# An inference step of a pooling and sparse-attention decoder: VectorE's steps reordered in the chosen-key loop, and block loads asked for one tile later

## The chip, the cores and the metric

The kernel is one program on 1 core of one Trainium2 chip. A core has TensorE (PE in the profile; its weight loads are PEld), VectorE (DVE), ScalarE (ACT), GpSimd (POOL) and SyncE (SP). Each takes its own instructions in the order written and they meet only at semaphores. SP, ScalarE and GpSimd also issue DMAs. The metric is the device time of one execution in microseconds, lower is better: 1763.3 us, the median of 3 runs (1761.06 to 1765.92).

## What is computed

One decoder layer works on 512 prompt rows and 8 sample rows (520 columns once transposed). The input is projected, pooled, attended in three branches, gated, merged, projected out and normalised. Cut to what matters here:

```python
h = x @ w_in + b_in              # u | z_pool | q | kv (6 parts) | gates | z_nsa | merge gates
# pooling: trailing means over 2, 4, 8, 16 positions, minus the token
c = cumsum(u);  m = (c[i] - c[i - w]) / min(pos + 1, w) - u
y_pool = (m per group @ pool_w) * pool_scale
# sparse attention of the 8 sample rows
p_cmp = masked_softmax(q . compressed_keys)           # 64 compressed blocks
score = p_cmp summed over the 4 heads of a group, and over 2 blocks; first and current block forced
idx   = top_k(score, 16)                              # 16 blocks of 64 keys
o_sel = softmax(q . k[idx]) @ v[idx]
o_win = softmax(q . window_keys) @ window_values      # 512 keys
o = g0 * o_cmp + g1 * o_sel + g2 * o_win
a = (y_pool * silu(z_pool)) @ w_up_pool;  b = (o * silu(z_nsa)) @ w_up_nsa
y = layer_norm(ALPHA * x + (sigmoid(gA) * a + sigmoid(gB) * b) @ w_out)
```

## The kernel before

**Units.** Every large projection is cut into units of 128 output columns. A weight tile (128x2048 f32, 1 MB) is loaded by SP into `wst`, ScalarE rounds it to `wh` (`split_hi`, L654), VectorE forms the remainder `wl` (`split_lo`, L659), and TensorE does three passes for each of 16 slices and two halves of the rows: 96 matmuls (L671 to L673). Two buffers alternate. A unit may be done in 8 parts of 12 matmuls, and `fill(count)` puts so many parts wherever TensorE would otherwise wait.

**The chosen-key loop.** The sample rows' attention runs in 48 steps t, between the parts of filler units. Steps 0 to 23 (`K_END`) are keys: 0 to 7 (`W_END` is 8) are window keys, 8 to 23 chosen keys, two steps to a sample row. Steps 24 to 47 are values. One key step is, on TensorE, `turn_keys(t)` (8 transposes, L938), `fill(FILL[t])` (2 or 3 parts) and `score_keys(t)` (4 matmuls, L955). After the transposes ScalarE rounds the turned keys (`out_keys`, L1343), VectorE subtracts (`out_keys`, L1678), and only then may `score_keys(t)` go. `ended(t)` names the filler unit that TensorE finishes in step t: this is one in the steps 0, 2, 5, 9, 12, 14, 17, 20 and 23, and none in the others. There `end_unit` does ScalarE's `split_hi` of the unit after next and the output of the ended one, and VectorE's `split_lo`; `split_hi` waits until TensorE has used the old weights.

**Other work in these steps.** VectorE ranks the blocks (`rank_blocks` at t = 1, `choose_blocks` at t = 3). At t = 5 it waits for TensorE's row of block offsets, copies it (L1818) and signals `gather_ready`, for which SP, GpSimd and ScalarE wait before they load the first chosen tile. From t = 8 it does the pooling of one u tile in two steps (`pool_tile`: even t the first half, odd t the second), and at t = 9 a chain of small operations, `row_gain` (L1734 to L1743).

**Chosen tiles.** Tile f is used by `turn_keys(f)` and lies in buffer f % 4. It consists of blocks of 64 rows, 32 KB each and two heads: SP and GpSimd issue six each, ScalarE the rest (`load_rest`: four for even f, two for odd f). ScalarE's issues stand between its `out_keys(t)` and its `end_unit`. The order of everything is written out by hand.

**The start.** After x has been turned and split, TensorE turns the first cache pages (L734, `turn_pages`), for which it waits for the semaphores `t_evac`, then begins unit 0.

Of the kernel before, what the change touches and what calls it, by code (L numbers as in the profile page):

```python
# [64 lines left out]
def build(nc, x_prompt, x_sample, cache_cmp_k, cache_cmp_v, cache_slc_k, cache_slc_v, cache_win_k,  # L65
# [5 lines left out]
    with ExitStack() as ctx:  # L71
        def sem(name):
            return ctx.enter_context(nc.semaphore(name))
# [114 lines left out]
        t_evac = [sem("t_evac0"), sem("t_evac1")]  # L188
# [59 lines left out]
        W_END, K_END, VW_END, V_END = 8, 24, 32, 48  # L248

        def parts_before(t):  # L250

            return 8 + sum(FILL[:t]) + (SEAM if t >= K_END else 0)

        def unit_fill(k):

            return k % 2, k // 2 + 27 - k % 2

        def ended(t):

            after = parts_before(t) + FILL[t] + (SEAM if t == K_END - 1 else 0)  # L260
            return range(parts_before(t) // 8 if t else 0, after // 8)
# [15 lines left out]
        def load_chosen(eng, regs, cache, n, h, first, last, signal):  # L277

            slot, base = n % 4, n // 2 * 32 + h * 16 + n % 2 * 8
            eng.load(regs[0:last - first], row_offs.bitcast(I32)[:, base + first:base + last])  # L280
            for r in range(first, last):
                at = eng.snap(regs[r - first], min_val=0, max_val=2 * NPHYS - 1)
                eng.dma_start(stage8[r % 2 * 64:r % 2 * 64 + 64, slot, r // 2, h * HD:(h + 1) * HD],
                              blocks_of(cache)[bass.ds(at, 1), :, h, :].rearrange("o p d -> p (o d)")
                              ).then_inc(signal[slot], 16)
# [363 lines left out]
        def split_hi(act, b, n, first=False, k=KD):  # L649

            act.wait_ge(w_in_s[b], n * 16 + 16)
            if not first:
                act.wait_ge(w_used[b], n)
            act.activation(wh[:, b, 0:k], wst[:, b, 0:k], ACT.Copy).then_inc(w_hi[b], 1)  # L654

        def split_lo(dve, b, n, k=KD):

            dve.wait_ge(w_hi[b], n + 1)
            dve.tensor_tensor(wl[:, b, 0:k], wst[:, b, 0:k], wh[:, b, 0:k].bitcast(F32), ALU.subtract).then_inc(w_lo[b], 1)  # L659
# [457 lines left out]
        def _(act):  # L1117
# [8 lines left out]
            for k in range(KD):  # L1126
# [2 lines left out]
            act.wait_ge(x_tr, KD + 2)  # L1129
            act.activation(xh[:, :, SEQ:ROWS], pb[5][:, 0:KD * NB].rearrange("p (k b) -> p k b", b=NB), copy  # L1130
                           ).then_inc(x_hi, 1)
            split_hi(act, 0, 0, first=True)
            act.sem_inc(phase, 1)

# [10 lines left out]

            for b in range(2):
                act.sem_inc(evac[b], 1)
            act.sem_inc(t_evac[1], 1)
            act.sem_inc(c2_evac, 1)
            for b in range(2):  # L1150
                act.sem_inc(spilled[b], 1)
# [173 lines left out]
            def load_rest(cache, n, last=8):  # L1325

                for h in range(NKV):
                    load_chosen(act, block_regs, cache, n, h, 6, last, k_in)
# [9 lines left out]
            def out_keys(t):  # L1338
                if t > 0:
                    act.wait_ge(sk_done, t)  # L1340
                for h in range(NKV):
                    act.wait_ge(kt_ready[h], t + 1)
                    act.activation(khl[:, 0, h, :], pb[4 + h][:, :], copy).then_inc(kh_ready, 1)  # L1343

            def move_low(bank, cols, scored):

                act.wait_ge(sk_done, scored)
                act.activation(S[:, cols], pb[bank][64:P, 0:cols.stop - cols.start], copy).then_inc(lo_moved, 1)
# [22 lines left out]
            for t in range(K_END):  # L1371
                if t == W_END:
                    move_low(6, slice(1024, 1536), W_END)
                out_keys(t)
                if t == 6:
                    act.wait_ge(gather_ready, 1)
                    load_rest(cache_slc_k, 0)
                if 6 <= t < K_END - 3:
                    load_rest(cache_slc_k, t + 3 - W_END, 8 - (t + 3) % 2)
                if t == K_END - 1:  # L1380
                    move_low(6, slice(0, 512), K_END - 1)
                    turned_hi(pTw, 5, WPG, 1)
                    values_hi(K_END)
                    move_low(7, slice(512, 960), K_END)
                for k in ended(t):
                    end_unit(k)
                if t == W_END:
                    exps(1, slice(1024, 1536), 1)
# [73 lines left out]
        def _(dve):  # L1462

            for k in range(KD):
# [3 lines left out]
            dve.wait_ge(x_hi, KD + 1)  # L1468
            dve.tensor_tensor(xl[:, :, SEQ:ROWS], pb[5][:, 0:KD * NB].rearrange("p (k b) -> p k b", b=NB),
                              xh[:, :, SEQ:ROWS].bitcast(F32), ALU.subtract).then_inc(x_lo, 1)  # L1470
            split_lo(dve, 0, 0)
            dve.sem_inc(phase, 1)

# [9 lines left out]
                last.then_inc(evac[b], 1)  # L1483


            dve.sem_inc(t_evac[0], 1)
            def compress_sequence(kv, r, par, first=False):
                n = r * 2 + (kv * NB + par)

# [179 lines left out]
            def end_unit(k):  # L1669
                b, n = unit_fill(k)  # L1670
                split_lo(dve, b, n + 1)
                if k >= 8:
                    silu_tile(u[:, k, :], b, k, k - 7)
# [125 lines left out]
            for t in range(K_END):  # L1799
                if t == W_END:  # L1800
                    add_high(6, slice(1024, 1536), 1)
                out_keys(t)
                if t == K_END - 1:
                    add_high(6, slice(0, 512), 2)
                    turned_lo(pTw, 5, WPG, 1)
                    dve.tensor_copy(wm[:, 8:16], pb[5][:, 256:264])
                    dve.drain().then_inc(pl_ready, 1)
                    values_lo(K_END)
                    add_high(7, slice(512, 960), 3)
                for k in ended(t):  # L1810
                    end_unit(k)
                if t == 1:
                    rank_blocks()
                if t == 3:
                    choose_blocks()
                if t == 5:
                    dve.wait_ge(step, C + 12)
                    dve.tensor_copy(row_offs.bitcast(I32), pb[7][0:1, 0:256])  # L1818
                    dve.drain().then_inc(gather_ready, 1)
                    dve.tensor_copy(osum, pb[7][:, 320:384])  # L1820
                    dve.drain().then_inc(step, 1)
                if t == W_END:
                    row_max(1, slice(1024, 1536))
                if t == W_END + 1:
                    row_gain(1, 1)
                if t >= W_END:
                    pool_tile((t - W_END) // 2, (t - W_END) % 2 == 1)
            for t in range(K_END, V_END):
                if t + 1 < V_END:
                    values_lo(t + 1)  # L1830
                if t - 1 >= K_END and (t <= VW_END or t % 2 == 0):
                    add_values(t - 1)
                if t == K_END:
                    row_max(0, slice(0, 960))
                if t == K_END + 4:
                    row_gain(0, 2)
                if t == K_END + 6:
                    turned_lo(pTs, 6, 8, 2)
                    dve.tensor_copy(wm[:, 0:8], pb[7][:, 128:136])
                    dve.drain().then_inc(pl_ready, 1)  # L1840
                if t == K_END + 7:
                    for kind in range(2):
                        dve.tensor_tensor(newv[:, kind * 64:kind * 64 + 64].rearrange("p (x g) -> p x g", g=G),
                                          pb[7][:, kind * 64:kind * 64 + 64].rearrange("p (x g) -> p x g", g=G),
                                          by_head(vnew, kind), ALU.mult)
                    dve.drain().then_inc(new_evac, 1)
                    for kind in range(2):
                        dve.tensor_tensor(osum, osum, newv[:, kind * 64:kind * 64 + 64], ALU.add)
                        dve.drain()
                for k in ended(t):  # L1850
                    end_unit(k)
                if t == VW_END + 7:
                    dve.wait_ge(sums_ready, 1)
                    dve.tensor_tensor(ssum, pb[6][:, 0:64].rearrange("p (c b) -> p c b", b=NB), u[:, 0:8, SEQ:ROWS], ALU.add)
                    dve.drain()
                    for g, w in enumerate(POOL_W):
                        new = u[:, 2 * g:2 * g + 2, SEQ:ROWS]
                        last = dve.scalar_tensor_tensor(new, ssum[:, 2 * g:2 * g + 2, :], 1.0 / w, new, ALU.mult, ALU.subtract)
                    last.then_inc(diff_ready, 1)
# [180 lines left out]
```

## Time and profile before

| What | Value |
|---|---|
| Median of 3 runs | 1763.3 us (1761.06 to 1765.92) |
| The profiled execution | 1766.08 us, of which the span is 1764.6 |
| Mean granted TensorE clock | 0.983 |
| PE busy | 1710.6 us (97% of the span) |
| DVE busy | 738.0 us (42%) |
| ACT busy | 582.7 us (33%) |
| POOL busy | 165.7 us (9%) |

Busy time is the time in which at least one instruction of the engine was running. The rows shown further down are from the same execution; all starts are microseconds from the start of its span. A row of the timeline gives the start, the duration in us, engine, line, operation, output and inputs, the count, and in brackets how long the engine had been idle before and whose end released it. ACTq, DVEq and the like are an engine's sequencer, which issues DMAs. The key steps 5 to 23 lie between 1026 and 1150 us.

### The profile page before, as it was taken

The numbers are of one execution on the slowest core, as the hardware profiler recorded it, in microseconds if no ns is written. First come the engines' busy times: TensorE is split into PE (matmuls) and PEld (weight loads), VectorE is DVE, ScalarE is ACT, GpSimd is POOL, SyncE is SP. The second block draws the span as 40 slices with busy tenths as digits, with TensorE's granted clock in tenths as the row PEclk, the third lists the DMA queues.
The fourth block names the chain that finished last, engine by engine and source line by source line (L and its number), as shares of the span: only waits on it lengthen the run. The fifth ranks groups of instructions, "written<-read, shape, count | busy, mean of one in ns | idle before, by whom it ended". The sixth has DMA issues, their size and how long they took to land.

```text
span 1764.6 us, 35960 instructions
## 1 busy us (share of the span) xinstructions
PE 1710.6 (97%) x13797; PEld 1662.1 (94%) x13797; DVE 738.0 (42%) x1169; ACT 582.7 (33%) x830; POOL 165.7 (9%) x320
## 2 busy tenths in 40 slices
PE   7999999999999998999999999989999999999996
PEld 6999999999999998998989988889999999999996
DVE  4333323222222113444544446564353444455685
ACT  4433333331222213333333332354232333343331
POOL 0000000000000010000000135236200000000000
PEclk9999999999999987999999999999999999999998
DMA  9555655544444254222322646456633444577783
GB/s 280 156 156 148 191 160 146 151 142 148 140 128 123 71 147 124 72 75 63 85 66 60 209 122 160 127 156 153 173 82 91 144 138 137 140 210 217 203 243 103
DMA packets 354262, 248.87 MB, mean 141 GB/s; under 512 B 16893, under 2 KB 336835, under 8 KB 353378
## 3 DMA queue, kind: packets, MB, share of 16 engines
q1 hardware_dynamic: 330114, 205.28, 41.6%
q0 software_dynamic: 15104, 38.81, 7.0%
q10 hardware_dynamic: 8960, 3.68, 0.8%
q8 instruction: 50, 0.82, 0.2%
q14 instruction: 34, 0.28, 0.1%
HBM read 229.50 MB, written 27.03 MB: 145 GB/s over the span
## 4 chain that ended last, share of the span: by engine, by line
PE 55%; DVE 3%; ACT 1%; DVEq 1%; issue 1%; ACTq 1%; PEldq 0%; PEld 0%
PE bank L671 8%; PE bank L672 8%; PE bank L673 8%; PE bank L1079 3%; PE bank L1080 3%; PE bank L1081 3%; PE bank L687 3%; PE bank L688 3%; PE bank L689 3%; PE bank L867 2%; PE bank L955 1%; PE bank L938 1%; DVE wl L659 1%; PE bank L851 1%; PE bank L837 1%; PE bank L839 1%
## 5 line engine op out<-in xcount | busy, mean ns | idle before, releaser
L671 PE MATMUL bank<-xh,wh 128*128 128x260 f32 x1952 | 563.2, 289 | 1.3 <-DVE wl L659 1.0
L672 PE MATMUL bank<-xl,wh 128*128 128x260 f32 x1952 | 553.2, 283 | 0.0
L673 PE MATMUL bank<-xh,wl 128*128 128x260 f32 x1952 | 552.9, 283 | 0.0
L659 DVE TENSOR_TENSOR wl<-wst,wh 128x2048 fp32r<-128x2048 f32 (+1 forms) x141 | 289.0, 2049 | 353.9 <-ACT wh L654 353.7
L671 PEld LDWEIGHTS bank<-xh,wh 128*128 128x128 f32 x1952 | 369.7, 189 | 2.7 <-DVE wl L659 1.2
L672 PEld LDWEIGHTS bank<-xl,wh 128*128 128x128 f32 x1952 | 369.7, 189 | 0.0
L673 PEld LDWEIGHTS bank<-xh,wl 128*128 128x128 f32 x1952 | 369.5, 189 | 0.0
L654 ACT ACTIVATE wh<-wst 128x2048 fp32r<-128x2048 f32 (+1 forms) x141 | 243.2, 1725 | 129.2 <-PE bank L673 101.8
L687 PE MATMUL bank<-xh,wh 128*128 128x260 f32 x512 | 155.3, 303 | 0.0
L1079 PE MATMUL bank<-xh,wh 128*128 128x264 f32 (+1 forms) x512 | 147.3, 288 | 0.0
L688 PE MATMUL bank<-xl,wh 128*128 128x260 f32 x512 | 145.2, 284 | 0.0
L689 PE MATMUL bank<-xh,wl 128*128 128x260 f32 x512 | 145.2, 284 | 0.0
L1081 PE MATMUL bank<-xh,wl 128*128 128x264 f32 (+1 forms) x512 | 144.4, 282 | 0.0
L672 PE MATMUL bank<-yl,wh 128*128 128x260 f32 x512 | 144.4, 282 | 0.0
L673 PE MATMUL bank<-yh,wl 128*128 128x260 f32 x512 | 144.3, 282 | 0.0
L671 PE MATMUL bank<-yh,wh 128*128 128x260 f32 x512 | 144.3, 282 | 0.0
L1080 PE MATMUL bank<-xl,wh 128*128 128x264 f32 (+1 forms) x512 | 144.3, 282 | 0.0
L754 PE MATMUL bank<-xt,w 128*128 128x128 f32 (+1 forms) x1024 | 118.2, 276 | 0.0
L754 PEld LDWEIGHTS bank<-xt,w 128*128 128x128 f32 x1024 | 115.6, 192 | 1.6
L644 ACT ACTIVATE xt<-bank 128x512 f32<-128x512 f32 x64 | 75.7, 1183 | 105.9 <-PE bank L734 105.7
L643 DVE COPY xt<-bank 128x512 f32<-128x512 f32 x64 | 73.7, 1152 | 82.7 <-PE bank L734 82.7
L687 PEld LDWEIGHTS bank<-xh,wh 128*128 128x128 f32 x512 | 97.4, 190 | 3.1 <-issue 1.9
(320 smaller groups left out, 2350.2 us busy)
## 6 DMA issues: line engine op xcount, KB each, us to landing
wst<-in_w_in SPq DMA_DIRECT2D x77, 1024.0 KB, 5.7
wst<-in_w_out SPq DMA_DIRECT2D x32, 1024.0 KB, 6.0
stage<-in_cache_cmp_k SPq DMA_DIRECT2D x128, 128.0 KB, 2.2
stage<-in_cache_cmp_v SPq DMA_DIRECT2D x128, 128.0 KB, 2.1
merge_gates<-sig POOLq DMA_DIRECT2D x32, 260.0 KB, 2.3
sig<-merge_gates POOLq DMA_DIRECT2D x32, 260.0 KB, 2.9
wst<-in_w_up_pool SPq DMA_DIRECT2D x16, 512.0 KB, 4.3
wst<-in_w_up_nsa SPq DMA_DIRECT2D x16, 512.0 KB, 4.2
```

What stands on the lines that cost most here:

```text
L654: act.activation(wh[:, b, 0:k], wst[:, b, 0:k], ACT.Copy).then_inc(w_hi[b], 1)
L659: dve.tensor_tensor(wl[:, b, 0:k], wst[:, b, 0:k], wh[:, b, 0:k].bitcast(F32), ALU.subtract).then_inc(w_lo[b], 1)
L671: pe.matmul(bank[:, 0:HALF], wh[:, b, k, :], hi[:, rows], start=(at == 0), stop=False)
L672: pe.matmul(bank[:, 0:HALF], wh[:, b, k, :], lo[:, rows], start=False, stop=False)
L673: last = pe.matmul(bank[:, 0:HALF], wl[:, b, k, :], hi[:, rows], start=False, stop=end)
L687: pe.matmul(bank, wh[:, b, k, :], xh[:, k, rows], start=(k == 0), stop=False)
L688: pe.matmul(bank, wh[:, b, k, :], xl[:, k, rows], start=False, stop=False)
L689: last = pe.matmul(bank, wl[:, b, k, :], xh[:, k, rows], start=False, stop=(k == KD - 1))
L754: last = pe.matmul(pb[6][:, 0:width], w1[:, j, :], xt[:, par, j, 0:width], start=(j == 0), stop=(j == CB - 1))
L1079: pe.matmul(bank[:, 0:width], wh[:, b, k, :], xh[:, k, rows], start=(k == 0), stop=False)
L1080: pe.matmul(bank[:, 0:width], wh[:, b, k, :], xl[:, k, rows], start=False, stop=False)
L1081: last = pe.matmul(bank[:, 0:width], wl[:, b, k, :], xh[:, k, rows], start=False, stop=(k == KD - 1))
```

## The change

Three edits. In VectorE's key loop, `end_unit` is moved from before the ranking, copying, `row_gain` and pooling work of the step to after it. In ScalarE's key loop, the rest of tile f is asked for in step f - 2 and no longer in step f - 3; tile 8's rest stays in step 6. At the start, the first increments of `t_evac` stand ahead of the first weight split on both engines and no longer behind it.

```diff
@@ scalar
             act.activation(xh[:, :, SEQ:ROWS], ...).then_inc(x_hi, 1)
+            act.sem_inc(t_evac[1], 1)
             split_hi(act, 0, 0, first=True)
...
-            act.sem_inc(t_evac[1], 1)
             act.sem_inc(c2_evac, 1)
@@ scalar, key loop
                 if t == 6:
                     act.wait_ge(gather_ready, 1)
-                    load_rest(cache_slc_k, 0)
-                if 6 <= t < K_END - 3:
-                    load_rest(cache_slc_k, t + 3 - W_END, 8 - (t + 3) % 2)
+                if 6 <= t < K_END - 2:
+                    load_rest(cache_slc_k, t + 2 - W_END, 8 - t % 2)
@@ vector
+            dve.sem_inc(t_evac[0], 1)
             split_lo(dve, 0, 0)
...
-            dve.sem_inc(t_evac[0], 1)
@@ vector, key loop
                     values_lo(K_END)
                     add_high(7, slice(512, 960), 3)
-                for k in ended(t):
-                    end_unit(k)
                 if t == 1:
                     rank_blocks()
...
                 if t >= W_END:
                     pool_tile((t - W_END) // 2, (t - W_END) % 2 == 1)
+                for k in ended(t):
+                    end_unit(k)
```

In the changed file the lines of VectorE's helpers are one lower (L1677 for L1678, L1783 to L1788 for L1784 to L1789, the first half of `pool_tile`). On VectorE at t = 14 and 15, before: keys of 14, weight split, first half of pooling, keys of 15.

```order
L1678 TENSOR_TENSOR khl<-bank,khl 128x512 x2
L659 TENSOR_TENSOR wl<-wst,wh 128x2048
L1784 COPY ukeep<-u 128x23
L1785 COPY u<-u 128x512
L1789 TENSOR_TENSOR u<-u 128x512 x2
L1678 TENSOR_TENSOR khl<-bank,khl 128x512 x2
```

And after, at the same place:

```order
L1677 TENSOR_TENSOR khl<-bank,khl 128x512 x2
L1783 COPY ukeep<-u 128x23
L1784 COPY u<-u 128x512
L1788 TENSOR_TENSOR u<-u 128x512 x2
L659 TENSOR_TENSOR wl<-wst,wh 128x2048
L1677 TENSOR_TENSOR khl<-bank,khl 128x512 x2
```

The split has gone from the front of the pooling to just ahead of the next step's keys. On ScalarE from its `out_keys(9)` to the split of weights in step 9, before:

```order
L1343 ACTIVATE khl<-bank 128x512 [waits kt_ready1]
L280 TENSOR_LOAD kc
L282 ISA
L283 DMA stage<-in_cache_slc_k 64x128
L282 ISA
L283 DMA stage<-in_cache_slc_k 64x128
L280 TENSOR_LOAD kc
L282 ISA
L283 DMA stage<-in_cache_slc_k 64x128
L282 ISA
L283 DMA stage<-in_cache_slc_k 64x128
L654 ACTIVATE wh<-wst 128x2048 [waits w_used1,w_in1]
```

And after:

```order
L1343 ACTIVATE khl<-bank 128x512 [waits kt_ready1]
L280 TENSOR_LOAD kc
L282 ISA
L283 DMA stage<-in_cache_slc_k 64x128
L280 TENSOR_LOAD kc
L282 ISA
L283 DMA stage<-in_cache_slc_k 64x128
L654 ACTIVATE wh<-wst 128x2048 [waits w_used1,w_in1]
```

The odd step now holds two DMAs ahead of the split where it held four; an even step holds four where it held two. TensorE's, GpSimd's and SP's own order is the same in both.

## Rows read from the trace of the kernel before

**Rows 1.** Waits, TensorE's own, 984 to 1165: waiter, releaser, total, times, longest.
```profile
PE bank L955 <- DVE khl L1678: 7.0, 5, 2.2
...
PE bank L1008 <- DVE stage8r L1754: 2.3, 1, 2.3
```

**Rows 2.** Timeline of TensorE: scores of steps 7, 10, 15 and 18.
```profile
1042.48 1.33 PE L955 MATMUL bank<-khl,qm 128*128 128x512 f32 x4 [1.29 <-DVE khl L1678]
...
1063.97 1.33 PE L955 MATMUL bank<-khl,qm 128*128 128x512 f32 x4 [2.24 <-DVE khl L1678]
...
1095.61 1.33 PE L955 MATMUL bank<-khl,qm 128*128 128x512 f32 x4 [1.91 <-DVE khl L1678]
...
1117.16 1.33 PE L955 MATMUL bank<-khl,qm 128*128 128x512 f32 x4 [0.73 <-DVE khl L1678]
```

**Rows 3.** Chain of waits, 1030 to 1046: start, us, what.
```profile
1034.57 0.36 DVEq L1819
...
1038.44 0.64 ACTq L283
...
1041.11 0.60 ACT khl L1343
```

**Rows 4.** Timeline of TensorE, step 5's last matmuls ahead of the offsets.
```profile
1030.17 1.05 PE L962 MATMUL bank<-kc,vc 64*128 64x4 f32 x8
```

**Rows 5.** Timeline of ScalarE, steps 9, 13 and 14.
```profile
1051.83 4.20 ACTq L283 DMA_DIRECT2D stage<-in_cache_slc_k  x4
1056.14 1.92 ACT L654 ACTIVATE wh<-wst 128x2048 fp32r<-128x2048 f32 x1 [4.37 <-issue]
...
1078.56 3.23 ACTq L283 DMA_DIRECT2D stage<-in_cache_slc_k  x4
...
1084.66 1.46 ACTq L283 DMA_DIRECT2D stage<-in_cache_slc_k  x2
1088.60 1.91 ACT L654 ACTIVATE wh<-wst 128x2048 fp32r<-128x2048 f32 x1 [3.69 <-PE bank L673]
```

**Rows 6.** Timeline of VectorE, steps 9 and 10, 14 and 15, 17, 23.
```profile
1058.09 2.29 DVE L659 TENSOR_TENSOR wl<-wst,wh 128x2048 fp32r<-128x2048 f32 x1 [5.60 <-ACT wh L654]
...
1063.22 1.29 DVE L1678 TENSOR_TENSOR khl<-bank,khl 128x512 fp32r<-128x512 f32 x2
...
1090.55 2.29 DVE L659 TENSOR_TENSOR wl<-wst,wh 128x2048 fp32r<-128x2048 f32 x1 [4.81 <-ACT wh L654]
...
1094.86 1.29 DVE L1678 TENSOR_TENSOR khl<-bank,khl 128x512 fp32r<-128x512 f32 x2
...
1112.36 2.29 DVE L659 TENSOR_TENSOR wl<-wst,wh 128x2048 fp32r<-128x2048 f32 x1 [5.16 <-ACT wh L654]
...
1153.31 2.29 DVE L659 TENSOR_TENSOR wl<-wst,wh 128x2048 fp32r<-128x2048 f32 x1 [0.62 <-ACT wh L654]
```

**Rows 7.** Stretches: length, busy of PE, PEld, DVE, ACT, POOL, granted clock, DMA.
```profile
26.00:32.00 6.00, 6.00 (x27) 6.00 (x28) 0.98 (x1) 0.20 (x1) 0.00 (x0) 0.50 0.86 246
1060.00:1070.00 10.00, 7.76 (x54) 6.56 (x53) 6.83 (x20) 1.20 (x2) 7.27 (x15) 1.00 0.49 137
...
1097.00:1101.00 4.00, 4.00 (x23) 4.00 (x22) 2.47 (x8) 1.20 (x2) 1.05 (x2) 0.57 0.78 175
```

**Rows 8.** Line L283, the issues of chosen keys, 984 to 1165.
```profile
DMA to landing us min/median/max: 1.9/2.6/6.4
```

**Rows 9.** Timeline of ScalarE, keys of step 18.
```profile
1112.95 1.08 ACT L1343 ACTIVATE khl<-bank 128x512 fp32r<-128x512 f32 x2
```

**Rows 10.** Timeline of TensorE, transposes of tile 20.
```profile
1123.53 1.04 PE L938 MATMUL bank<-ident,stage 128*128 128x128 f32 x8
```

**Rows 11.** Waits of all engines, 1160 to 1290.
```profile
ACT khl L1368 <- DMA stage<-in_cache_slc_v: 31.2, 10, 5.4
```

**Rows 12.** Timeline of TensorE, the start.
```profile
23.93 1.07 PE L734 MATMUL bank<-ident,stage 128*128 128x128 f32 x8 [2.42 <-DVEq L1486]
26.00 0.58 PE L671 MATMUL bank<-xh,wh 128*128 128x260 f32 x1 [1.00 <-DVE wl L659]
```

## The prediction

> **What bounds the kernel now.** The table of engines comes first: TensorE is busy for 97% of the span and the next engine for 42%, so only what makes TensorE wait, or runs it at a lower clock, moves the end. I then read the waits of TensorE alone over the stretch of the key steps [rows 1]. One line stands out: the score matmuls L955 waited five times for VectorE's `khl`, 7.0 us in all. Just behind the stretch, L1008, the first value products, waited once for 2.3. No wait of TensorE on a tile's DMA is in this answer, so the chosen tiles come in time.
>
> Next, TensorE's timeline around each of the five [rows 2]: 1.29 us at step 7, 2.24 at step 10, 1.91 at step 15, 0.73 at step 18, and by difference from the 7.0 some 0.8 for the fifth, at step 21, which follows the same pattern as step 18. All but step 7 come right after a step in which a filler unit ends (9, 14, 17, 20). That points to `end_unit`.
>
> **Part 1: VectorE's order in the key steps.** Nothing is added or removed; seven splits (steps 5, 9, 12, 14, 17, 20, 23) go behind the other work of their steps. Take step 14 [rows 6]: the split `wl` starts at 1090.55 after 4.81 us of idle time, in which VectorE waited for ScalarE's `wh`. It takes 2.29 us, to 1092.84. Then comes the pooling, to 1094.86, where the keys of step 15 begin. Pooling depends on neither `wh` nor the keys, so it fits into the 4.81 us. With it there, keys 15 start at about 1092.85, 2.0 us sooner, and the score can start at 1093.6. TensorE was ready at 1095.61 - 1.91 = 1093.70 [rows 2]. The stall goes, by a margin of only 0.1.
>
> Steps 17 and 20 have the same shape: idle of 5.16 us ahead of the split at 17 [rows 6], whose end is 1114.65. Keys 18 could then start at once, and the score 0.75 us later (in rows 2 and 6 the score of step 10 starts 1063.97 - 1063.22 = 0.75 after its keys), at 1115.4, against a TensorE ready at 1117.16 - 0.73 = 1116.43. Stall gone, margin 1.0. I take step 20 to be the same, 0.8.
>
> Step 9: the split ends at 1060.38 and `row_gain` with the second half of pooling fill the time to keys 10 at 1063.22 [rows 6]: 2.8 us, which fit into the 5.60 idle ahead. TensorE was ready at 63.97 - 2.24 = 1061.73; keys at 1060.4 mean a score at 1061.15. Gone, margin 0.6 even before part 2.
>
> Step 5: the copy behind `gather_ready` waits for TensorE's offsets, whose matmuls end at 1031.2 [rows 4]. Before, it stood behind the split and its signal came at 1034.57 + 0.36 = 1034.93 [rows 3]. Now it comes at about 1031.2 + 0.4, the same 0.36 with a hand-over, 1031.6: 3.3 us sooner, for ScalarE, SP and GpSimd alike. The first chosen blocks are thus asked for earlier, with the queues of these three empty.
>
> At step 23 the split waited 0.62 for `wh` [rows 6]; 2.5 us of pooling can start in that time, so what follows, up to the values that L1008 awaits, is 0.5 earlier of its 2.3 [rows 1]. Its stall stays at 1.8.
>
> What is late now: `wl` itself, by up to the part of the pooling that doesn't fit. The next use of that buffer lies one whole unit, 8 parts of 12 matmuls, further on, so TensorE doesn't notice; nor does SP, which reloads the buffer after it.
>
> Sum of part 1, with step 7 left to part 2: 2.24 + 1.91 + 0.73 + 0.8 + 0.5 = 6.2 us.
>
> **Part 2: ScalarE's requests.** The count stays 48; each batch of two or four moves one step back. At step 6 ScalarE issued six behind `gather_ready`, and its `khl` began at 1041.11, VectorE's behind it, and the score at 1042.48 [rows 2, 3]. Now it issues four. The first four ended at 1038.44 + 0.64 = 1039.08 [rows 3], and with the signal sooner they can only end sooner. Then the first head's keys 7 on ScalarE, 0.55 (half of 1.08, rows 9), and on VectorE, 0.7 (half of 1.29 and the hand-over, rows 6), and the score may go at 1040.4, against a TensorE ready at 1042.48 - 1.29 = 1041.19. The 1.29 go.
>
> From step 9 on, odd steps issue two and even steps four; before it was the reverse. Step 9 gains: four took 4.20 us and held `wh` until 1056.14 ("issue" is the releaser) [rows 5]. Two save about 2, more margin at step 10. Steps 12, 14 and 20 lose: four take 3.23 in the row of step 13, two take 1.46 at step 14, so 1.8 more in front of `wh`. At 14 the issues would end at 1084.66 + 3.23 = 1087.9, and `wh` waits for TensorE to finish the unit until 1088.60 anyway [rows 5]: hidden, by 0.7. With a batch as slow as that of step 9 (4.20) it would be 0.3 late. So these steps cost from 0 to 0.3 each; I take 0 and keep up to 1 us for the three together.
>
> The price of asking late is the landing. The tightest tile is 20: ScalarE ends keys 18 at 1114.03 [rows 9], four issues bring 1117.4, and the median landing of 2.6 us [rows 8] brings 1120.0. TensorE turns tile 20 at 1123.53 [rows 10]. That leaves 3.5 us, or 2.8 when the 0.73 of step 18 is gone. The longest landing, 6.4, would be late by 1.0. I take 0, bound 1.
>
> Here the Trainium skill speaks against the change: DMA: Bandwidth & Descriptors, Rules for kernel authors, says in effect that a DMA should be issued early and its semaphore waited for late, so that its fixed cost overlaps. By it the later request is at best neutral. The trace has slack of more than a median landing, which is why I give the rule only a small chance; its result is the slower rival below.
>
> Part 2: 1.3 us.
>
> **Part 3: the start.** TensorE's page transposes ran at 23.93, released by VectorE's semaphore increment behind its split, and unit 0 began at 26.00 when `wl` was there [rows 12]. The transposes were already beside the split. They can go sooner, by at most the 2.42 us of idle ahead of them, but the first matmul waits for the same `wl`: 0. What can move is the clock. After the idle stretches of 2.42 and 1.00 it stood at 0.50, the 1.2 GHz level, from 26 to 32 [rows 7]. At half rate 6 us do 3 us of work. Had it stayed at full, 3 us would be won; if it lasted half as long again, 1.5 lost. The idle time is nearly the same, merely more of it in one piece before unit 0; I take 0.
>
> The skill's rule (TensorE: Matmul & The Clock Gate, Part 1) is that a busy engine is given the full clock and an idle one the half, and that the place of the change differs between runs. It gives no sign for this part, and a rival below.
>
> **The clock in the loop.** From 1097 to 1101 the granted clock was 0.57 [rows 7], that is 2 x 0.43 x 4 = 3.4 us at the half level, right behind the 1.91 us stall of step 15. That cost 1.7 us. But the longer stall of step 10 was followed by nothing, 1.00 [rows 7]. So a stall leads to the lower clock sometimes. Without stalls the 1.7 should return, though shifting everything may put another stall, such as the one of 1.8 left at L1008, in its place. Between 0 and 1.7 I take 1.0.
>
> **Sum.** 6.2 + 1.3 + 0 + 1.0 = 8.5 us. The profiled execution took 1766.08, its span 1764.6, and is 2.8 above the median 1763.3, at the upper end of the runs. It would become 1757.6; against the median, 1763.3 - 8.5 = 1754.8 us.
>
> **Rivals.**
> 1. ScalarE's even steps become the bound. Margins of 0.1 and 0.7 at steps 14 and 15 are thin. If four issues there take as long as the slow batch of step 9 and more, `wh`, `wl` and keys 15 are late and part of the 1.91 comes back, with the clock's 1.0: 8.5 - 1.9 - 1.0 - 0.8 (the same at step 21) = 4.8, giving 1758.5. For: rows 5 show a spread of 3.23 to 4.20. Against: only step 9's was so slow, with SP and GpSimd at work in a crowd that now comes earlier.
> 2. The value steps take it back. ScalarE waited ten times, 31.2 us, for chosen values [rows 11]. If those were bound by the rate of DMA, a TensorE that comes 8 us earlier would wait there. Against: TensorE itself shows no such wait, and these loads start by TensorE's own progress. It would leave 1 or 2 us: 1762.
> 3. Slower: rests land late. One tile later, with four issues in the even steps, leaves 2.8 us over the median landing at tile 20. If landings there pass 2.6 + 2.8 = 5.4 us, TensorE waits at its transposes. If seven even tiles waited 2 us each, 14 us against the 8.5: 1763.3 + 5.5 = 1768.8. For: a longest landing of 6.4. Against: a median of 2.6. This is the skill's early-issue rule.
> 4. The clock at the start. With all else as forecast, 3 us either way: 1751.8 at full clock throughout, 1756.3 if the low level lasts longer.
>
> **Chances.** Forecast 0.64, rival 1 0.16, rival 2 0.11, rival 3 0.05, rival 4 0.04. The forecast's own bounds: 6.2 + 1.3 with 1 lost to ScalarE and no clock is 6.5, with the 1.7 of the clock and a little more elsewhere 10.5, and the median itself moves by 1: 1752 to 1758. The range takes in rivals 1 and 4 and runs towards 2: 1750.5 to 1761.5. A change is told from none here from about 0.3%, 5.3 us, so below 1758.0. Faster: nearly all of the forecast and rival 4, and a third of rival 1, 0.72. Slower, above 1768.6: 0.04. The same: 0.24.
>
> **What would show it.** Right: among TensorE's waits, L955 on `khl` falls from 7.0 to under 1; pooling stands before the split, in the idle time; the first chosen DMA is issued at about 1032; the clock is 1.00 from 1060 to 1150. L1008's wait is about 1.8. Part 2 is wrong if TensorE's transposes wait for a DMA, or if ScalarE's `wh` in steps 12, 14 or 20 has "issue" as its releaser with a stall of L955 behind it. The forecast is wrong if the stalls vanish and the time doesn't, for then they were not on the path; or if another stall of like size stands in the value steps.

## The result, and the profile after

| | Before | Changed |
|---|---|---|
| Median | 1763.91 us (5 runs, 1761.06 to 1765.92) | 1753.89 us (5 runs, 1753.21 to 1756.05) |
| Ratio | | 0.9945, 95% interval 0.9934 to 0.9957 |
| Span profiled | 1764.6 us | 1752.0 us |

The change makes the kernel 10.0 us faster by the medians and 0.55% (9.7 us) by the ratio; the forecast was 1754.8. A second set of five runs beside other kernels gave 1755.67 with a ratio of 0.9946 (0.9932 to 0.9959). One execution of the kernel before, beside the second group of experiments below, took 5133 us and is left out of its ratios.

TensorE's waits over the key steps and just behind them in the changed kernel, 984 to 1155, in the columns of [rows 1]:

```profile
PE bank L1008 <- DVE stage8r L1753: 1.6, 1, 1.6
PE bank L1008 <- DVE osacc L1761: 0.6, 1, 0.6
```

The line of L955 with its 7.0 us isn't there any more; L1008 stands at 1.6 where it had 2.3. VectorE's timeline at steps 14 and 15, to be laid beside [rows 6]:

```profile
1078.00 1.29 DVE L1677 TENSOR_TENSOR khl<-bank,khl 128x512 fp32r<-128x512 f32 x2 [2.80 <-ACT khl L1343]
1079.21 0.17 DVE L1783 COPY ukeep<-u 128x23 f32<-128x23 f32 x1
1079.28 0.42 DVE L1784 COPY u<-u 128x512 f32<-128x512 f32 x1
1079.78 1.46 DVE L1788 TENSOR_TENSOR u<-u 128x512 f32<-128x512 f32 x2
1084.06 2.29 DVE L659 TENSOR_TENSOR wl<-wst,wh 128x2048 fp32r<-128x2048 f32 x1 [2.82 <-ACT wh L654]
1086.27 1.28 DVE L1677 TENSOR_TENSOR khl<-bank,khl 128x512 fp32r<-128x512 f32 x2
```

The pooling lies in the idle time ahead of the split, which falls from 4.81 to 2.82 us, and the keys of step 15 follow the split at once. TensorE's score of that step has no bracket, that is, its first matmul did not wait:

```profile
1087.07 1.27 PE L955 MATMUL bank<-khl,qm 128*128 128x512 f32 x4
```

But it took 1.27 us where most take 1.07 to 1.09. A score is two pairs of matmuls, one for each head, and the second pair needs the second half of VectorE's keys. TensorE's weight loads (PEld) show that wait, which the matmul row doesn't:

```profile
1087.60 0.30 PEld L955 LDWEIGHTS bank<-khl,qm 128*128 128x128 f32 x2 [0.30 <-DVE khl L1677]
```

The waits of the weight loads on `khl` from 1026 to 1150, before and changed:

```profile
PEld bank L955 <- DVE khl L1678: 10.0, 12, 2.4
...
PEld bank L955 <- DVE khl L1677: 0.3, 1, 0.3
```

Before, both pairs waited in six steps: the five of [rows 1] and step 6, whose matmul row took 1.33 us without a bracket. In the changed kernel one pair is left, that of step 15.

VectorE in step 5, the copy behind `gather_ready` ahead of the split:

```profile
1029.64 0.41 DVE L1815 CAST kc<-bank 1x256 int32<-1x256 f32 x1 [2.31 <-PE bank L962]
```

ScalarE in steps 6, 9, 12 and 14, to be laid beside [rows 5]:

```profile
1032.53 3.16 ACTq L283 DMA_DIRECT2D stage<-in_cache_slc_k  x4
...
1047.88 1.77 ACTq L283 DMA_DIRECT2D stage<-in_cache_slc_k  x2
1049.75 1.92 ACT L654 ACTIVATE wh<-wst 128x2048 fp32r<-128x2048 f32 x1 [1.73 <-PE bank L673]
...
1065.64 3.11 ACTq L283 DMA_DIRECT2D stage<-in_cache_slc_k  x4
1068.85 1.92 ACT L654 ACTIVATE wh<-wst 128x2048 fp32r<-128x2048 f32 x1 [3.16 <-issue]
...
1078.41 3.10 ACTq L283 DMA_DIRECT2D stage<-in_cache_slc_k  x4
1082.11 1.91 ACT L654 ACTIVATE wh<-wst 128x2048 fp32r<-128x2048 f32 x1 [3.66 <-PE bank L673]
```

Step 9's `wh` is released by TensorE and no longer by the issues. In step 12 it is now the issues that hold it ("issue"), as the price of four in an even step, but no score waits behind. In step 14 the four end at 1081.51, 0.6 ahead of TensorE's release.

The start of each score, read from TensorE's timelines, shows where the time went. A line holds a step, its start in both kernels and by how much the changed kernel is ahead:

| Step | Before | Changed | Ahead | Wait of the step before the change |
|---|---|---|---|---|
| 5 | 1031.15 | 1029.53 | 1.6 | |
| 7 | 1042.48 | 1039.00 | 3.5 | 1.29 |
| 9 | 1055.46 | 1051.71 | 3.8 | |
| 11 | 1069.42 | 1062.99 | 6.4 | 2.24 (step 10) |
| 14 | 1088.34 | 1081.85 | 6.5 | |
| 15 | 1095.61 | 1087.07 | 8.5 | 1.91 |
| 16 | 1103.55 | 1093.37 | 10.2 | |
| 19 | 1122.61 | 1111.31 | 11.3 | 0.73 (step 18) |
| 23 | 1147.89 | 1135.41 | 12.5 | 0.80 (step 21) |

In this pair of executions 10.9 us are gained between steps 5 and 23. The 1.6 ahead of step 5 were there at the score of step 0 already (998.20 and 996.59), before anything that the loop's edits move, and the start edit gives nothing by itself, as the third experiment shows. From step 15 to 16 another 1.6 us are gained with no wait: that is the stretch in which the clock stood at 0.57 [rows 7] and now stands at 1.00.

### The profile page after: what moved, and what is told of

Same layout as the page of the kernel before. It is cut to its first block, busy times and chain, and to the rows that moved or that the text cites. A ratio compares the mean times of both kernels' runs of the same rounds, so it can differ in the third digit from the quotient of the medians.

```text
span 1752.0 us, 35960 instructions
## 1 busy us (share of the span) xinstructions
PE 1706.5 (97%) x13797; PEld 1659.8 (95%) x13797; DVE 737.1 (42%) x1169; ACT 583.2 (33%) x830; POOL 165.9 (9%) x320
## 4 chain that ended last, share of the span: by engine, by line
PE 58%; DVE 2%; DVEq 1%; issue 1%; ACT 0%; PEldq 0%; ACTq 0%; PEld 0%
PE bank L671 9%; PE bank L672 8%; PE bank L673 8%; PE bank L1079 4%; PE bank L1080 3%; PE bank L1081 3%; PE bank L687 3%; PE bank L688 3%; PE bank L689 3%; PE bank L867 2%; PE bank L938 1%; PE bank L955 1%; PE bank L851 1%; PE bank L837 1%; PE bank L839 1%; PE bank L1056 1%
## 5 line engine op out<-in xcount | busy, mean ns | idle before, releaser
L643 DVE COPY xt<-bank 128x512 f32<-128x512 f32 x64 | 73.9, 1155 | 81.5 <-PE bank L734 81.5
```

## The experiments

Twelve runs in three groups; within a group all ran on one chip beside runs of the kernel before. Ratios are to the kernel before.

**Parts alone.** Each with only its part of the diff shown ahead.

VectorE's order alone:

```diff
-                for k in ended(t):
-                    end_unit(k)
...
                     pool_tile((t - W_END) // 2, (t - W_END) % 2 == 1)
+                for k in ended(t):
+                    end_unit(k)
```

> Kernel before with only VectorE's new order in the key steps. Theory (stalls of the scores, each costing its idle time and about 0.4 us more): the waits of steps 10, 15, 18 and 21 go, 5.7 us of idle, 4 x 0.4 for restarting and up to 1.7 of clock, and 0.7 at L1008; step 7 keeps at most 0.3, since gather_ready comes 3.3 us sooner though ScalarE still issues six. Total -8 to -10.5 us, ratio 0.9943 to 0.9955; L955 waits under 0.5 in all. Rival (ScalarE's requests are what frees steps 7 and 10): step 7 keeps its 1.3 and step 10 about 2, total -5, ratio 0.997.

Measured: 1755.06 us, ratio 0.9956 (0.9943 to 0.9969). No matmul row of L955 has a wait. The scores of steps 5 to 23 lie 106.17 us apart; 116.74 before and 105.88 in the whole change. At step 6 ScalarE still issues six:

```profile
1033.30 5.07 ACTq L283 DMA_DIRECT2D stage<-in_cache_slc_k  x6
1038.47 1.09 ACT L1343 ACTIVATE khl<-bank 128x512 fp32r<-128x512 f32 x2 [5.34 <-issue]
```

The keys of step 7 are held by the issues, but these begin sooner, since `gather_ready` comes sooner. The score of step 7 starts 0.1 late, its second pair waits 0.30 for the second head (in the weight loads), and by step 8 0.3 us are lost, which is the whole difference to the 105.88. So this part alone is nearly the whole gain.

ScalarE's requests alone:

```diff
-                    load_rest(cache_slc_k, 0)
-                if 6 <= t < K_END - 3:
-                    load_rest(cache_slc_k, t + 3 - W_END, 8 - (t + 3) % 2)
+                if 6 <= t < K_END - 2:
+                    load_rest(cache_slc_k, t + 2 - W_END, 8 - t % 2)
```

> Kernel before with only ScalarE's later requests. Theory: step 7's wait goes (1.3 and 0.4), step 10's falls from 2.2 to 0 to 0.3 because wh comes 2 us sooner; steps 15, 18, 21 keep 1.9, 0.7, 0.8. Total -3 to -4.5 us, ratio 0.9975 to 0.998. Together with the run of VectorE's order alone this is more than the whole change, as steps 7 and 10 are freed by either. Rival (the two edits add up): about -2 us, ratio 0.999.

Measured: 1760.83 us, ratio 0.9989 (0.9981 to 0.9998), 1.9 us by the ratio (0.4 to 3.4) and 3.0 by the medians, where 3 to 4.5 were expected. In the profile the scores of steps 5 to 23 lie 113.41 us apart, 3.3 less than before. TensorE's timeline, all waits of L955, at steps 13, 15, 18 and 21:

```profile
1078.62 1.33 PE L955 MATMUL bank<-khl,qm 128*128 128x512 f32 x4 [0.31 <-DVE khl L1677]
1092.23 1.32 PE L955 MATMUL bank<-khl,qm 128*128 128x512 f32 x4 [1.89 <-DVE khl L1677]
1113.81 1.33 PE L955 MATMUL bank<-khl,qm 128*128 128x512 f32 x4 [0.73 <-DVE khl L1677]
1132.99 1.33 PE L955 MATMUL bank<-khl,qm 128*128 128x512 f32 x4 [0.81 <-DVE khl L1677]
```

Steps 7 and 10 are free, as expected; but step 13 has a new wait of 0.31, which neither theory had. It is the price of four issues in step 12, with split and pooling still in the old order. The time leaves both theories open (1.9 is what the rival said, 3.3 what the first did); the waits decide for the first: either part frees steps 7 and 10 by itself, so their gains can't be added.

The start alone:

```diff
+            act.sem_inc(t_evac[1], 1)
             split_hi(act, 0, 0, first=True)
...
+            dve.sem_inc(t_evac[0], 1)
             split_lo(dve, 0, 0)
```

> Kernel before with only the start edit. Theory: nothing in time, within 1 us, ratio 0.9995 to 1.0005: TensorE's first unit waits for wl in any case. Rival (the start edit gave the 1.6 us that the profile of the whole change was ahead by before the key steps, through the clock or an earlier first unit): -1.6 us, ratio 0.9991, with unit 0's first matmul or the end of the 1.2 GHz stretch 1 us or more sooner.

Measured: 1764.8 us, ratio 1.0006 (0.9996 to 1.0016). Nothing. And both loop parts without the start:

> The whole change without the start edit. Theory: as the whole change, 1753 to 1755 us, ratio 0.9938 to 0.9952, no wait of L955. Rival (start edit worth 1.6 us): 1755.5, ratio 0.9955.

Measured: 1754.23 us, ratio 0.9953 (0.9939 to 0.9967), no wait of L955, 105.87 us from the score of step 5 to that of 23. The start edit is worth nothing that these runs can tell; the 1.6 us ahead of the loop are most likely a difference between executions. Even among profiles whose code is the same up to there, the score of step 5 stood between 1027.70 and 1033.16. In the changed kernel the transposes do start sooner, now released by the page's DMA and no more by VectorE, and unit 0 still waits for `wl`:

```profile
22.71 1.89 PE L734 MATMUL bank<-ident,stage 128*128 128x128 f32 x8 [1.94 <-DMA stage<-in_cache_cmp_k]
...
25.32 0.58 PE L671 MATMUL bank<-xh,wh 128*128 128x260 f32 x1 [0.72 <-DVE wl L659]
```

**Margins and their price.** Work put back behind the split of steps 9, 14, 17 and 20 in the changed kernel, its result unused:

```diff
                 for k in ended(t):
                     end_unit(k)
+                if t in (9, 14, 17, 20):
+                    for _ in range(4):
+                        dve.tensor_tensor(sig[:, 1, 0:SEQ], u[:, 0, 0:SEQ], u[:, 0, 0:SEQ], ALU.add)
+                        dve.drain()
```

> The changed kernel with four idle additions of 128x512 (0.69 us each, one after the other, about 2.9 us in all) on VectorE behind the weight split of steps 9, 14, 17 and 20, so that the next keys come 2.9 us later. From the changed kernel's trace the margins of the scores are 3.0 us at step 10, 0.1 at 15, 1.0 at 18 and 1.5 at 21, so waits of 0, 2.8, 1.9 and 1.4 come back, 6.1 us. Theory (a stall costs its idle time and about 0.4 us more, and sometimes the clock): +7.3 us, up to +9 with the clock, against the changed kernel, 1761 to 1763. Rival (a stall costs what its wait shows): +6.1 us. Second rival (the margins are wrong, since the next step's work is hidden elsewhere): under +3 us.

Measured: 1763.63 us, ratio 1.0000 (0.9991 to 1.0009): 9.7 us over the changed kernel. TensorE's timeline:

```profile
1088.48 1.32 PE L955 MATMUL bank<-khl,qm 128*128 128x512 f32 x4 [2.86 <-DVE khl L1677]
...
1109.66 1.33 PE L955 MATMUL bank<-khl,qm 128*128 128x512 f32 x4 [1.95 <-DVE khl L1677]
...
1132.40 1.33 PE L955 MATMUL bank<-khl,qm 128*128 128x512 f32 x4 [1.42 <-DVE khl L1677]
```

The stretch behind the second wait (busy time and count of PE, PEld, DVE, ACT and POOL, SP, then granted clock, DMA share and GB/s):

```profile
1110.00:1120.00 10.00, 10.00 (x50) 8.65 (x49) 4.92 (x11) 1.53 (x3) 3.14 (x6) 0.66 0.46 113
```

The margins were right to 0.1 us: 2.86, 1.95 and 1.42 for 2.8, 1.9 and 1.4, and no bracket at step 10, where only the second pair of the score waited. The price was higher than the theory. In the profile, steps 5 to 23 take 116.26 us, 10.4 more than 105.88, for 6.2 us of waits. About 2.9 of it is the clock: 0.66 over 10 us is 6.8 us at the 1.2 GHz level, right behind the second wait, and from the score of step 18 to that of 19 it is 8.37 us, against 5.45 in the kernel before, where step 18 waited too and the clock stayed up. The rest, 1.2, is 0.2 to 0.4 for each of the four steps that were held.

One such wait alone, three additions in step 14:

> The changed kernel with three idle additions (2.2 us) behind the weight split of step 14 alone: the margin of 0.1 makes one stall of 2.1 us at step 15, like the 1.91 of the kernel before. Theory (idle time and about 0.3 more, and in some executions 1.7 of clock): +2.4 to +4.1 us, and the scores of steps 14 to 17 lie 2.4 further apart in the profile, or 4.1 with the clock below 1.00 behind them. Rival (the clock falls behind every such stall): 4.1 always; other rival (cost is the idle time alone): +2.1.

Measured: 1755.87 us, ratio 0.9950 (0.9936 to 0.9963), against 1755.67 and 0.9946 for the changed kernel beside it. TensorE's timeline:

```profile
1091.12 1.96 PE L955 MATMUL bank<-khl,qm 128*128 128x512 f32 x4 [2.07 <-DVE khl L1677]
```

The stretches around and behind the wait:

```profile
1090.00:1094.00 4.00, 2.88 (x10) 2.35 (x11) 2.43 (x6) 0.00 (x0) 1.11 (x3) 0.66 0.86 237
1094.00:1100.00 6.00, 6.00 (x46) 5.80 (x45) 3.46 (x8) 1.19 (x2) 3.33 (x6) 0.94 0.58 145
```

In the profiled execution, which took 1760.23, the wait of 2.07 cost 3.75 us from step 14 to step 19, about 1.5 of it through the clock (3.4 us at the low level; from the score of step 15 to that of 16 it is 7.84 us, against 6.30 in the changed kernel). But the medians hardly differ, and the intervals overlap: the expected 2.4 to 4.1 are neither shown nor excluded in the time. Sorted by mean clock it is clearer. At 0.985 the one kernel took 1754.99, 1755.10 and 1755.87, the other (one run) 1753.44: 1.6 to 2.4 more. "Always 4.1" doesn't fit: the fastest of these three less 4.1 would be a changed kernel at 1750.9, and the fastest of its ten runs took 1753.21.

Five times the changed kernel again, for that comparison:

> The changed kernel once more, beside the three that follow, so that they are compared on one chip: 1753 to 1756 us, no wait of L955, waits of 1.6, 0.55 and 1.75 us at L1008.

Measured: 1755.67 us, with the expected waits.

Requests yet one step later:

```diff
                     act.wait_ge(gather_ready, 1)
-                if 6 <= t < K_END - 2:
-                    load_rest(cache_slc_k, t + 2 - W_END, 8 - t % 2)
+                    load_rest(cache_slc_k, 0)
+                if 8 <= t < K_END - 1:
+                    load_rest(cache_slc_k, t + 1 - W_END, 8 - (t + 1) % 2)
```

> The changed kernel with ScalarE's requests yet one step later (tile f asked for in step f - 1; tile 8 as before). Theory (the margin of a tile is the time from ScalarE's issue to TensorE's transposes less the landing of 2.6 us): even tiles, with four issues, would be late by 1.5 to 2.5 us, odd tiles, with two, in time or late by under 0.5. Seven even tiles make 10 to 17 us of TensorE's waits at L938 and more from restarting and the clock: 1765 to 1776. Rival (landing is hidden by the filler parts, as it starts with the first issue): under +3 us, 1757.

Measured: 1782.05 us, ratio 1.0107 (1.0091 to 1.0123), 28 over the changed kernel and 6 over the upper end that was expected. Its waits, and the longest, at tile 16, with ScalarE's last requests for it:

```profile
PE bank L938 <- DMA stage<-in_cache_slc_k: 18.3, 8, 4.7
```

```profile
1106.18 1.75 PE L938 MATMUL bank<-ident,stage 128*128 128x128 f32 x8 [4.67 <-DMA stage<-in_cache_slc_k]
```

```profile
1098.66 2.31 ACTq L283 DMA_DIRECT2D stage<-in_cache_slc_k  x3
```

All even tiles from 10 on came late (tile 18 by only 0.3), and of the odd ones tile 9. The requests for tile 16 ended at 1100.97 and the tile was there at 1106.18, 5.2 us later and not 2.6. The waits are 18.3 us; what they add to the scores of steps 5 to 23 is 26.2, so almost 8 more: the granted clock stood at 0.79 for the 8 us behind four of the eight waits (1.90, 2.53, 4.67 and 2.93), which is 1.7 us each, and at 1.00 behind the others. The expectation took the median landing for each tile. The nine block DMAs issued by all engines between 1097.9 and 1101, around ScalarE's last for tile 16, landed in 4.4 us by their median and 5.7 at most, while the median of the whole loop was 2.4; SP had asked for a 1 MB weight tile at 1099.60. A tile needs the last of its 14 or 16 DMAs, and just there they are slow. That the weight tile is what slows them was not tested. The change has used up most of the slack that there was; one step more would lose more than twice what it won.

**Towards a better version.** The last half of the pooling out of step 23 into step 34:

```diff
-                if t >= W_END:
+                if W_END <= t < K_END - 1:
                     pool_tile((t - W_END) // 2, (t - W_END) % 2 == 1)
...
+                if t == VW_END + 2:
+                    pool_tile(7, True)
```

> The changed kernel with the last half of the pooling (2.5 us on VectorE) taken out of step 23 and done in step 34. Theory (VectorE's chain up to the values of step 25 sets the wait of L1008, 1.6 and then 0.55 us): both waits go, with 0.4 each for restarting, -2.5 to -3 us, 1751. Rival (ScalarE's values, two table loads and the exponentials are next): under -1 us.

> The kernel with the last half of the pooling in step 34, once more. Theory: the wait of 1.6 us at L1008 is gone and the two behind it stay, -1.6 to -2.0 us against the changed kernel. Rival (the earlier difference of 1.7 us was one between sessions): within 0.5 us of it.

Measured: 1752.24 us, 0.9937 (0.9925 to 0.9949), and the second time 1751.13 us, 0.9925 (0.9912 to 0.9939), beside 0.9946 for the changed kernel. It is the fastest of all by the medians. Beside the changed kernel it was 4.5 us faster, where 1.6 to 2.0 were expected, though the intervals of the two ratios overlap; between runs at the same mean clock of 0.985 it is 2.3 to 2.8 (1750.61 to 1751.13 against 1753.44). TensorE's waits of L1008 in it:

```profile
PE bank L1008 <- DVE osacc L1761: 2.3, 2, 1.7
```

The 1.6 is gone; the two others stay. The first expectation was wrong in its mechanism, as the 0.55 isn't from that chain. What the second left out is the clock: over the 8 us behind the wait of 1.75 it stood at 1.00 in both profiles of this kernel, and at 0.79 in both of the changed one, which is 1.7 us. That it will always do so can't be said from two profiles.

The end of unit 9 put off from step 28 to step 29, in addition:

```diff
-                for k in ended(t):
+                for k in () if t == K_END + 4 else ended(t - 1) if t == K_END + 5 else ended(t):
                     end_unit(k)
```

> The same, and VectorE's end of unit 9 (weight split and gating, 3.2 us) moved from step 28, where row_gain stands too, to step 29. Theory: the wait of step 30 for osacc, 1.75 us, followed by the clock at 0.83 in that stretch, goes too: another -2 to -4 us, 1747 to 1749.5. Rival (the wait moves to step 31, since VectorE's work is only shifted by 2.4 us): no more than the run before, 1751.

Measured: 1755.55 us, 0.9954 (0.9941 to 0.9967): 3 slower than without, and 4.5 over the rival's 1751. The one wait of 1.75 became two, of 1.01 and 2.06 us, and a further one of 1.05 on `stage8r` stands at 1188.30. TensorE's timeline, the two:

```profile
1161.75 0.38 PE L1008 MATMUL bank<-khl,pTw 128*128 128x256 f32 x1 [1.01 <-DVE osacc L1761]
...
1166.45 0.38 PE L1008 MATMUL bank<-khl,pTw 128*128 128x256 f32 x1 [2.06 <-DVE osacc L1761]
```

The rival was right in its mechanism: the wait moved. Then `row_gain` two steps sooner instead:

```diff
-                if t == K_END + 4:
+                if t == K_END + 2:
                     row_gain(0, 2)
```

> The same, and row_gain (six small operations of VectorE, 1.35 us) at step 26 in place of step 28, where VectorE was idle for 1.6 us. Theory (VectorE's queue, row_gain and the end of unit 9 in one step, sets the wait of 1.75 us at step 30): that wait falls to about 0.4, -1.4 to -1.7 us, and up to 1.7 more where the clock fell behind it: 1748.5 to 1751. Rival (it moves to another step, as with the end of unit 9 put off): no gain, 1752.3.

Measured: 1751.3 us, 0.9926 (0.9912 to 0.9939), the same as without. The waits are

```profile
PE bank L1008 <- DVE osacc L1761: 1.4, 2, 0.8
PE bank L1008 <- DVE stage8r L1753: 0.8, 1, 0.8
```

instead of 2.3: 1.75 fell to 0.84 where 0.4 was expected, and a new one of 0.8 stands at 1187.92. Again moved, not removed. What holds the value steps is thus not a single misplaced piece of VectorE's work; what does is left open.

## Why the prediction was right

**The reading.** That TensorE's five waits on `khl` were the change's whole gain, and all on the path, was right: their brackets are gone, and the table of scores has each of them. A sixth step, 6, was held too, by 0.4 us, and the prediction didn't see it.

**Part 1.** Its mechanism and margins held. At step 15 the margin was put at 0.1 and the added work of 2.9 us made a wait of 2.86. That margin is the first head's; for the second head there was none, and the step still loses 0.2 us (6.30 us from the score of step 15 to that of 16, against 6.13 from 11 to 12 and from 19 to 20). `gather_ready`'s copy now follows the offsets at once, as forecast, and the first chosen DMA is issued at 1031.3, forecast 1032; measured from the score of step 5 it comes 2.9 us sooner, forecast 3.3. L1008 went down by 0.7, forecast 0.5. The pooling after the split shows nothing late.

**Part 2.** 1.3 us were put down to the requests, for step 7. That is the attribution that failed: VectorE's order alone frees step 7 as well, by the earlier signal, even with six issues. The prediction's own numbers had it: a signal 3.3 us sooner is more than the wait of 1.29. The sum was unharmed, since the term was counted once. What this part adds to the other is 0.3 us in the profile (106.17 against 105.87 from score to score), and in the ratios 0.9956 against 0.9953, whose intervals overlap: nothing that can be told. That the even steps would cost 0 was right in the whole change, and wrong with the old order of VectorE (0.31 at step 13).

**The landing.** 2.8 to 3.5 us of slack at tile 20: in the changed kernel, ScalarE's issues for it end at 1105.99 (1103.32 + 2.67) and the transposes start at 1112.22, 6.2 less the median landing of 2.5, so 3.7 are left; less the longest landing of that stretch, 4.7, it is 1.5. The advice of the Trainium skill (DMA: Bandwidth & Descriptors, Rules for kernel authors) to issue a DMA early did not bite here (the later requests alone gave 0.9989), and did at the very next step, by 28 us.

**The start.** 0, as forecast.

**The sizes.** 6.2 and 1.3 for the stalls were 7.0 of wait and 0.5 at L1008; measured in the profile they are 9.3 between steps 5 and 23 without the clock's 1.6. The term that was too small is the cost of a wait, which the prediction put at its bracket alone: each of the six steps cost about 0.4 us more, for the reasons in the last section. At step 18 a wait of 0.73 cost 1.13 up to step 19 (12.46 us from the score of step 17 to that of 19 before, 11.33 now), at step 21 0.80 cost 1.2. The clock's term was 1.0, in the profile 1.6. It is not in every execution: the start-only kernel, which has the loop of the kernel before, waited 1.91 at step 15, kept its clock, and took 6.36 us to the next score instead of 7.94; its steps 5 to 23 took 114.48 us instead of 116.74. By the rounded mean clocks of the runs in the last group, 0.9827 before (nine) and 0.9836 for the changed kernel (five), it is 0.0009 x 2 x 1764 / 2 = 1.6 us too, though a step of that rounding, 0.001, is 1.8 us. Together 8.5 against 10.0, with an interval of 7.6 to 11.6. That the forecast lies within it is owed to the margins and mechanism; that it lies 1 us from the median is in part luck, since the clock's share differs between executions.

**The rivals.** None came. The nearest was ScalarE's even steps: its issues do hold `wh` in step 12 now.

## What to carry to other kernels

In an in-order queue, put the work that waits for nothing ahead of the instruction that waits for another engine, and read the fit beforehand: the idle time ahead of the waiting instruction against the work behind it, and the margin by what the bottleneck's own wait says of when it was ready. Two edits that free the same wait don't add up; try each alone before both are kept. A request may be moved later only by the slack to its last landing, read where the queues are fullest, and a wait of the bottleneck that is merely shifted comes back as another.

## What the runs showed of the hardware that was not expected

**A wait costs more than its bracket, and the rows say why.** The score matmuls take 1.33 us behind a wait and 1.07 to 1.09 in most steps without one, and a waiting score costs about 0.4 us beyond the idle time shown. About 0.24 of it is the second pair of the score, which waits in turn for VectorE's second half. In the kernel before at step 15:

```profile
1096.21 0.30 PEld L955 LDWEIGHTS bank<-khl,qm 128*128 128x128 f32 x2 [0.30 <-DVE khl L1678]
```

From the start of that score to the next transposes it is 1.17 us, in the changed kernel at step 14, where nothing waits, 0.93. The other 0.16 is how the bracket is counted: it begins at the end of the matmul before, which is 0.28 us long, while without a wait the score starts 0.12 after that matmul's start. So it is this program's two halves and the profile's way of counting; nothing here shows a cost of restarting the engine.

**The clock follows short waits, but not always.** The waits of 1.91 (before), 1.89 (requests alone), 2.07 and 1.95 (with work added) were followed by the 1.2 GHz level, in the last case for 6.8 us, which cost about 2.9 us, more than the wait; those of 2.24 and 2.86 weren't, nor was the 1.91 at step 15 in the start-only kernel, whose clock stood at 1.00 there. The length of a wait alone thus doesn't say it. The level behind the wait of 1.75 at step 30 stood at 0.83 over 10 us in both kernels, and at 1.00 in the kernels of the start and of the requests alone and in both profiles with the pooling in step 34. In the changed one it is this stretch:

```profile
1160.00:1170.00 10.00, 8.25 (x59) 8.13 (x59) 7.65 (x15) 3.02 (x4) 6.99 (x15) 0.83 0.90 217
```

The Trainium skill (TensorE: Matmul & The Clock Gate, Part 1) has it that the place of the change varies from run to run; the runs here agree: in the two profiles of the changed kernel the clock stood at 0.50 and at 0.61 between 23 and 26 us.

**Much of the spread between executions goes with this clock.** Of nine runs of the kernel before, the one at a mean clock of 0.985 took 1761.34 us and those at 0.982 took 1765.00 to 1766.19. 0.003 of 1764 us are 10.6 us at half speed, 5.3 us of time; they differ by 3.7 to 4.9.
